# Two blocks of the second modulation group ahead of the context mixer, three per mixer block in its loop

## What is computed

```python
silu_c, silu_cc = jax.nn.silu(c), jax.nn.silu(c_ctx)
for i in range(DEPTH):                                   # DEPTH = 2
    mod_x = (silu_c @ ada_w[i] + ada_b[i])[:, None, :]   # 1024 -> 6 x 1024
    mod_c = (silu_cc @ ada_w[i] + ada_b[i])[None, None, :]
    sh1, sc1, g1, sh2, sc2, g2 = jnp.split(mod_x, N_MOD, axis=-1)
    csh1, csc1, cg1, csh2, csc2, cg2 = jnp.split(mod_c, N_MOD, axis=-1)
    xn = _modulate(_rmsnorm(x, norm1_g[i]), sh1, sc1)
    cn = _modulate(_rmsnorm(h_ctx, norm1_g[i]), csh1, csc1)
    # layer 0: chunk mixer, of x and of the context
    #   z = gelu(h @ w_in); u, v = split(z); v = layernorm(v)
    #   v = w_s @ v + b_s (per 128 rows and group); out = (u * v) @ w_out
    # then: + g1 * y, then the expert stage (peer) of the second norm, + g2 * that
```

## Time and profile before

| | |
|---|---|
| median of 3 runs | 3670.94 us (3668.19 to 3677.93) |
| the profiled execution: its own time | 3678.18 us |
| its span | 3676.3 us |
| PE, busy | 2841.4 us (77%) |
| DVE, busy | 2319.3 us (63%) |
| ACT, busy | 1388.8 us (38%) |
| POOL, busy | 857.1 us (23%) |
| group L499 (PE, modulation blocks): busy; idle just before | 65.2 us; 62.1 us, of which 59.4 for W<-in_ada_w |
| slices 2 to 4 of 40 (92 to 368 us): PE busy; granted TensorE clock | 9, 8, 7 tenths; 9, 8, 7 tenths |

### The profile page before, as it was taken

The page is one execution under the profiler, slowest core; times in us unless marked ns, Lnnn a source line. Parts: engine busy times, 40 slices in busy tenths (PEclk is TensorE's granted clock), DMA queues, the critical chain, the costliest instruction groups (busy, mean ns, idle before and its releaser), DMA issues. The chain is left out here.

```text
span 3676.3 us, 53010 instructions
## 1 busy us (share of the span) xinstructions
PE 2841.4 (77%) x19024; PEld 1691.0 (46%) x19024; DVE 2319.3 (63%) x5182; ACT 1388.8 (38%) x3564; POOL 857.1 (23%) x780
## 2 busy tenths in 40 slices
PE   4987788778776887785566767677667989889898
PEld 3876244233222433331045622222115789777897
DVE  5843766868777666678634467777762259513397
ACT  1212434434443434443334233344432247423275
POOL 0001343334333433333400134344440000000000
PEclk7987899999988888886677899999867999999999
DMA  8885999999999999999946599999992325332353
GB/s 320 308 308 226 413 421 420 420 420 414 420 418 388 421 412 415 414 415 359 390 167 223 208 421 420 421 412 420 417 413 109 120 104 183 137 118 106 122 183 120
DMA packets 177278, 1153.11 MB, mean 314 GB/s; under 512 B 21877, under 2 KB 30477, under 8 KB 43421
## 3 DMA queue, kind: packets, MB, share of 16 engines
q0 software_dynamic: 111632, 810.60, 53.8%
q1 hardware_dynamic: 58460, 321.68, 23.4%
q10 hardware_dynamic: 6960, 17.93, 1.3%
HBM read 1128.86 MB, written 21.27 MB: 313 GB/s over the span
## 5 line engine op out<-in xcount | busy, mean ns | idle before, releaser
L1217 PE MATMUL PS<-AR 64*64 64x512 f32 x6144 | 984.8, 720 | 540.9 <-ACT AR L1275 538.0
L1384 DVE CUSTOM_DVE_ANT_0 AR<-AR,H 128x1024 f32<-128x1024 f32 x768 | 938.6, 1224 | 560.4 <-DMA AR<-in_peer_uv,AR 553.9
L1408 POOL DMA_INDIRECT AR<-in_peer_uv,AR x768 | 852.5, 1110 | 1674.1 <-PE PS L1217 1157.6
L1217 PEld LDWEIGHTS PS<-AR 64*64 64x64 f32 x6144 | 179.6, 147 | 989.3 <-ACT AR L1275 875.4
L1270 ACT ACTIVATE SM<-SM 128x1 f32<-128x1 f32 x768 | 155.5, 203 | 1211.3 <-DVE SM L1384 1210.5
L1176 PE MATMUL PS<-HT,W 128*128 128x256 f32 x1408 | 463.3, 440 | 2.0 <-issue 1.3
L1176 PEld LDWEIGHTS PS<-HT,W 128*128 128x128 f32 x1408 | 245.2, 202 | 435.4 <-issue 419.1
L1275 ACT ACTIVATE AR<-AR,SM 128x64 f32<-128x64 f32 x768 | 267.2, 348 | 26.2 <-PE PS L1217 1.1
L2625 PE MATMUL PS<-XP,WP 128*128 128x256 f32 x2112 | 263.8, 287 | 13.1 <-ACT WP L2771 7.0
L2625 PEld LDWEIGHTS PS<-XP,WP 128*128 128x128 f32 x2112 | 262.6, 196 | 15.6 <-issue 7.3
L1272 ACT ACTIVATE SM<-SM 128x1 f32<-128x1 f32 x768 | 226.3, 295 | 25.0
(11 more groups left out here) (368 smaller groups left out, 3410.8 us busy)
## 6 DMA issues: line engine op xcount, KB each, us to landing
W<-in_ada_w SPq DMA_DIRECT2D x48, 1024.0 KB, 7.9
W<-in_peer_w_q SPq DMA_DIRECT2D x44, 1024.0 KB, 9.2
W<-in_ffn_out SPq DMA_DIRECT2D x22, 1024.0 KB, 4.8
W<-in_ffn_gate SPq DMA_DIRECT2D x20, 1024.0 KB, 4.8
W<-in_ffn_val SPq DMA_DIRECT2D x20, 1024.0 KB
W<-in_cm_w_in SPq DMA_DIRECT2D x16, 1024.0 KB, 8.8
AR<-min_scr SPq DMA_DIRECT2D x16, 1024.0 KB, 7.1
AR<-in_peer_uv,AR POOLq DMA_INDIRECT x768, 15.8
```

Of the source, the lines that this page charges most:

```text
L1217: mm = pe.matmul(PS[c * self.HP:(c + 1) * self.HP, 4 + (u % 2) * 2 + half, :], self.DIAG[rows_, r % 4, :], self.UV[rows_, r % RING, D + c ...
L1384: v.tensor_tensor_reduce(rows_, rows_, H[:, self.tb(u), :], 1.0, 0.0, ALU.mult, ALU.add, self.ACTV[:, u % 2, k:k + 1]).then_inc(u_used.sem, 1)
L1408: g.indirect_dma_start(out=self.UV[:, r % RING, :], out_offset=None, in_=t["peer_uv"], in_offset=bass.IndirectOffsetOnAxis(ap=self.IDS[:, ...
```

## The change

Blocks of the modulation groups are spread differently over PE's order, and their loads over SP's.

- Ahead of `norm1c` PE does only blocks 0 and 1 of `ada[1]`, not all eight.
- In the mixer's loop three blocks follow each `pe_in(b)`, two of them ahead of `prep.pe` and one behind it, counted on from block 2 of `ada[1]`. The last two of these 24 are blocks 0 and 1 of `ada[4]`.
- In `pe_mix` stand blocks 2 and 3 of `ada[4]`, behind `pe_turn` blocks 4 and 5, and none behind `prep.pe(5)`.
- SP's loads follow the same count. ACT's `store` of `ada[1]` and `ada[2]` and DVE's `add_bias` of `ada[1]`, `ada[2]` move later.

```diff
@@ first_sync
-            for b in range(2, 8):
-                ada[1].load(b)
-            for b in range(7):
-                for at in (2 * b, 2 * b + 1):
-                    ada[2 + at // 8].load(at % 8)
+            for b in range(8):
+                for at in range(10 + 3 * b, 13 + 3 * b):
+                    ada[at // 8].load(at % 8)
                 if b + 2 < 8:
                     mixc.load_in(b + 2)
...
-            for b in (6, 7):
-                ada[3].load(b)
             mixc.load_ws()
             mixc.load_out(0)
...
-            for b in range(6):
+            for b in range(2, 6):
                 ada[4].load(b)
@@ first_pe
             drain(ada[0].pe())
-            drain(ada[1].pe())
+            drain(ada[1].pe(blocks=range(2)))
             pe.wait_ge(con_in, 16)
             drain(norm1c.pe())
             for b in range(8):
                 drain(mixc.pe_in(b))
-                at = 2 * b % 8
-                drain(ada[2 + b // 4].pe(blocks=range(at, at + 2)))
+                for at in (10 + 3 * b, 11 + 3 * b):
+                    drain(ada[at // 8].pe(blocks=range(at % 8, at % 8 + 1)))
                 if b in (1, 2, 4, 5, 7):
                     prep.pe((1, 2, 4, 5, 7).index(b))
-            drain(mixc.pe_mix(lambda: drain(ada[4].pe(blocks=range(0, 2)))))
+                at = 12 + 3 * b
+                drain(ada[at // 8].pe(blocks=range(at % 8, at % 8 + 1)))
+            drain(mixc.pe_mix(lambda: drain(ada[4].pe(blocks=range(2, 4)))))
             drain(mixc.pe_turn())
-            drain(ada[4].pe(blocks=range(2, 4)))
+            drain(ada[4].pe(blocks=range(4, 6)))
             prep.pe(5)
-            drain(ada[4].pe(blocks=range(4, 6)))
@@ first_act
             drain(norm1c.turned())
-            ada[1].store()
...
             drain(mixc.act_in(2))
+            ada[1].store()
             matrices(1)
             drain(mixc.act_in(3))
             mixc.act_sums()
-            ada[2].store()
...
             drain(mixc.act_in(4))
+            ada[2].store()
             matrices(2)
@@ first_dve
             drain(norm1c.apply())
+            some(26)
             ada[1].add_bias()
-            some(42)
-            ada[2].add_bias()
+            some(16)
             mixc.dve_means()
...
             drain(mixc.dve_apply(0))
+            ada[2].add_bias()
             some(30)
```

## The result

The changed kernel takes 3691.57 us (median of 6 runs, 3687.11 to 3705.82). The kernel before took 3672.48 in 6 runs beside it. The ratio is 1.0056, with a 95% interval of 1.0044 to 1.0068. It is slower by 19.1 us, outside the forecast range of 3662 to 3684. The profiled execution took 3687.11 with a span of 3685.3, which is 8.9 above the one of before.

The account below looks back on a forecast made before the run. The prediction took PE's nearly gapless front, its late start and ACT's delay behind the fifth chunk to bound the kernel. Terms +13.2 (up to pe_mix), -8.1 and -3.5 gave +1.6 on 3670.94, stated as 3673 us, range 3662 to 3684.

Parts of the forecast that it names:

- b: Between in(0) and the start of pe_mix: seven more modulation blocks at 0.985 each, +6.9 us.
- d: Behind the three new load waits in the loop: the clock falls and slows the next blocks, 3 x 1.7 = +5.1 us.
- f: From pe_mix on: nothing changes until prep.pe(5) ends, then out(0) follows at once, -8.1 us.
- (1): Ahead of the mixer: 7.2 us lie between norm1c's data being ready and PE taking it.
- (3): Behind the fifth chunk: PE waits 6.53 us for ACT's copies, a delay starting from the chunk's end wherever it lies.
- a: Ahead of norm1c: six blocks leave, in(0) starts 10.1 earlier, less 1.2 for the lower clock, -8.9 us.
- c: Third block in a row at b = 0, 3, 6: waits 4.2 each for its load, less present waits, +9.2 us.
- rival B: Loop: third-block loads land at 8.9 us, each wait grows by 3.8, +13.0 in all, 3684; chance 0.12.
- rival D: Slow in-blocks behind chunks get faster with a modulation block between, -2.9 in all, 3668; chance 0.05.
- e: Chunk 2: ACT's store of ada[2] now stands ahead of the chunk's copies, so the chunk waits +0.9 us.
- X: The start of pe_mix, at 200.74 in the kernel before; forecast to move by +13.2 us.
- g: Out loop: the late load of 2.72 and slow blocks go, out(0) runs 0.9 slower, together -3.5 us.

Follow-up runs that it names:

- e3: Changed kernel with six blocks of ada[1] ahead of norm1c instead of two, a third block only behind chunks 1, 2, 4 and 5; 3671.8 us, 0.9994 of the kernel before.
- a2: The changed kernel unchanged, profiled a third time; 3689.8 us, 1.0043 of the kernel before.
- a1: The changed kernel unchanged, profiled a second time; 3689.9 us, 1.0047 of the kernel before.
- e5: Changed kernel with four long unread matmuls in each of the three waits behind b = 0, 3 and 6; 3688.9 us, 1.0035 of the kernel before.
- e6: Changed kernel's later half alone: eight blocks ahead of norm1c, two more in the loop, none ahead of out(0); 3676.4 us, 1.0007 of the kernel before.
- e3b: e3 repeated unchanged for a second profile; 3673.0 us, 0.9993 of the kernel before.
- e1: Changed kernel with at most two modulation blocks in a row and the store of ada[2] behind chunk 2; 3680.6 us, 1.0018 of the kernel before.
- e12: Changed kernel's earlier half, no three blocks in a row, the kernel before's order from pe_mix on, ada[2] store behind chunk 2; 3684.5 us, 1.0027 of the kernel before.
- e8: e3 with the store and bias of ada[2] moved behind chunk 2; 3665.4 us, 0.9973 of the kernel before.
- e2: Changed kernel with the second of three blocks behind b = 0, 3 and 6 multiplied three times more; 3702.2 us, 1.0074 of the kernel before.

## Why the prediction was wrong, step by step

The step that failed is the price of the loop, b to d: +23.3 from in(0) to the end of the fifth chunk was forecast, +28.7 was measured in the pair and +32.6 as the mean of three. That is 9 of the 13 us by which the mean front, +14.7, misses the forecast of +1.6. Step f failed too, and in its mechanism, but it is worth only 1.3 in the pair and 1.9 as a mean.

*What bounds the kernel.* (1) is right, with one thing missed: the 7.2 us between ready and taken don't need all six blocks gone. The last two suffice; the others run while the norm's data is awaited (`e3`, in(0) at 74.0). (3) isn't right as it stands. ACT's delay behind the chunk's end was 11.1, 11.4 and 11.8 in before, and 8.1, 9.1 and 8.8 in after; it isn't the same wherever the end lies.

*a* was right to 0.3: in(0) at 72.8, and +1.5 for the clock instead of +1.2 (+2.0 in `a2`).

*b and c.* Seven more blocks, and the waits for loads. b counts blocks at 0.985, and that holds only where the clock is full. c said 4.2 at each of three places (5.1 less 0.985 is 4.1). The first two are 4.37 and 4.44, the third 6.38: its load was issued at 192.59 and used at 199.98, 7.4 us, with ACT's transfers of a chunk issued from 181.98 to 192.08. In `a1` and `a2` they are 4.03, 5.24, 5.69 and 3.97, 4.56, 4.35. And c let the loop's other waits vanish without a row that says so; 1.04 and 0.56 stayed, 2.9 in `a1`. Together +13.2 instead of +9.2, +12.7 as a mean. This is rival B's mechanism, in part and well below its price.

*d* was right in mechanism, as `e5` shows, and too low in price. The blocks and in-blocks behind the three waits cost 7.8 us in the pair and 7.3 as a mean, not 5.1. The trace of before had a nearer row than the 2.72 that d went by. It stands behind the out loop, a wait of 4.13 with dense work on both sides:

```profile
284.23 1.97 PE L894 MATMUL PS<-CON,AR 128*128 128x128 f32 x8 [4.13 <-ACT AR L866]
285.99 6.88 PE L900 MATMUL PS<-AR 128*128 128x32 f32 x32
```

At full clock these take 1.09 and 3.66.

d also put nothing for a second source of slow stretches, behind the chunks. In before an in-block stands there and is slow at some (8.84, 10.04). The prediction's rival D hoped that a modulation block between would mend that. Mostly the slow stretch only moved: in the pair those four in-blocks took 31.2 instead of 34.6, and as a mean 32.6 instead of 33.4, while the added blocks ahead of them cost 2.2 more than at full clock in the pair and 3.0 as a mean.

Behind the wait of 4.37 the granted clock was 0.50, and the blocks behind all three waits took 1.89. The Trainium skill, "TensorE: Matmul & The Clock Gate", section on HAM oscillation, describes a loop that waits for a DMA in each round and re-throttles each time; this trace agrees at the three waits. No run here shows that it covers the falls behind the chunks, where PE hadn't been idle for more than 1.1 us.

*e* was right in size, 1.1 more in chunk 2. But it is no constant: 2.18 here, 3.62 in `e6`, 4.00 in `e3b`.

*f* was wrong in its mechanism. "Behind X nothing changes up to the end of `prep.pe(5)`", and the 24th block "falls behind X and into ACT's delay". Neither is so. The block stands ahead of X and takes 1.8, and the waits for the loads of the two behind it (3.60, 1.81) took over from ACT: the second half of `pe_mix` starts 4.8 later than ACT's copies would let it (3.1 and 3.9 in `a1` and `a2`). ACT's shorter delay hid 3.0 of that. From there to out(0) it is 15.0 instead of 23.6, so the two blocks taken away gave what was forecast, and -6.8 is left instead of -8.1. `e1` and `e12`, with two blocks in that place instead of one, show the wait bare, 9.68 and 9.48; `e3` and `e8`, with none, hardly have it. I had read the 6.53 behind ACT as room, without asking when the loads of the blocks in it would be issued and land. `e6` shows the 8.1 itself to be right where that doesn't bind.

*g* -3.3 instead of -3.5 in the pair, but as a mean of three each it is 68.6 against 70.2, -1.6. A new wait of 1.74 behind out(1) is part of that; in `a1` and `a2` out(2) behind it also took 9.07.

*The base.* The forecast started from a median, 7.2 below the profiled time, as if the difference were a constant. It is a draw. The front of the first profile was 2.0 above before's mean, and after's first 4.2 below its own mean: 6 us of the loss were hidden in the first pair.

The miss of 17.5 in the medians is thus, in the pair: 5.4 in the loop (waits 4.0, modulation blocks 2.4, the in-blocks -0.7, the rest rounding), 1.3 behind it, 0.2 in the out loop and 0.4 behind the query. Other executions add some 6 to this pair's front, 3.8 of it in the loop, mostly slow clock. That makes some 13.5; the last 4 are no more than a kernel differs from itself. The chance of 0.11 for slower was too low. The range took in the ends of single steps one at a time, and c, d, f and g all came out on the slow side.

The signs that had been named for a wrong prediction didn't come: the three waits lay between 3 and 7, the clock fell behind them, and the added wait in the chunks was 1.1, near the 0.9 priced. What did tell it were the later places: X at 221.2 instead of 214, out(0) at 248.0 instead of 241.

**What stays open.** Why the clock falls behind some chunks and not behind others, in the same kernel and from one execution to the next. In `e8` the first chunk has the same wait of 1.10 and the same instructions as in after, and the block behind it takes 1.07. Every such fall stands in or behind a chunk, which is 16 transposes and 32 matmuls of 32 columns (L894, L900); no run changed the chunk itself. Nor is it shown how much of the loads' lateness in `pe_mix` is a late issue (the slot, or SP's order) and how much ACT's transfers beside them; where a load was issued late, the transfers were always under way. An `e1` or an after with SP's loads of `ada[4]` put ahead of those of the mixer would tell.

## What to carry to other kernels

When work is moved out of the way of a late start, move only what delays it: the part that runs while the start's data is awaited is free where it is, and costs its full time (and its loads' waits) where it goes. A wait that ends last on one engine is room for another operation only when that operation's own load has been traced back to the slot it needs, its place in the issuing engine's order, and the traffic it lands in. When the clock behind a wait is priced, take the longest slow stretch on record, not only the nearest wait. And where executions of one kernel differ by more than the effect, take three profiles of each before a ledger is believed; here the first pair showed 8.5 of the 14.7 us that the front lost.

## What the hardware showed that I had not expected

PE can stand still with nothing awaited that the profile shows. In `e2`, in bursts of some 170 to 300 small matmuls and as many weight loads, it did so for 4.24, 3.95 and 2.32 us. That it ran short of instructions is my reading; no run shows it. The kernel before has the same in its opening blocks, and so have both its repetitions (2.21 and 2.63):

```profile
51.47 1.23 PE L499 MATMUL PS<-W,SM 128*2 128x64 f32 x34 [2.62 <-issue]
```

The granted clock fell to 0.50 while PE was fully busy (106 to 110 us of after, above) behind chunks whose longest idle time was 1.10, and rose again by itself within 4 us.
